# A pooling and attention mixer on 8 cores: far masks queued ahead of the rope products, and the conditioning product on four 32-column quarters of the array

## What is computed

```
shift, scale, gate = split(silu(c) @ w_mod + b_mod)       # w_mod is 1024 x 3072, f32; also for c_ctx
h = rms_norm(x, g_pre) * (1 + scale) + shift               # the same for the context tokens
xa, ga, q, k, v, gb, gm = split(h @ w_in)                  # 1024 x 5632
y_a = pool_mixer(xa) * silu(ga)
y_b = windowed_attention(rope(q), rope(k), v, k_ctx, v_ctx, sink) * silu(gb)
out = (sigmoid(gm_a) * (y_a @ w_a) + sigmoid(gm_b) * (y_b @ w_b)) @ w_out
x_new = x + gate * rms_norm(out, g_post)
```

## Time and profile before

| | us |
|---|---|
| median of 3 runs | 2377.49 (2376.29 to 2379.74) |
| the profiled execution | 2375.37 |
| its span on the slowest core, from the first to the last instruction | 2373.8 |
| spans of all cores | 2366.8 to 2373.8 |
| TensorE busy | 2257.8 |
| VectorE busy | 1595.3 |
| ScalarE busy | 1150.0 |
| GpSimd (POOL) busy | 773.6 |

### The profile page before, as it was taken

How to read it: one execution, slowest core, us unless ns; L and a number is a source line. 1 busy time by engine, 2 the same in 40 slices (tenths; PEclk the granted TensorE clock), 3 DMA queues, 4 the chain that set the end, 5 groups by cost and what they waited for, 6 DMA issues and landing times.

```text
span 2373.8 us, 67010 instructions; the slowest of 8 cores (2366.8 to 2373.8 us)
## 1 busy us (share of the span) xinstructions
PE 2257.8 (95%) x23952; PEld 1336.5 (56%) x23952; DVE 1595.3 (67%) x4226; ACT 1150.0 (48%) x2341; POOL 773.6 (33%) x982
## 2 busy tenths in 40 slices
PE   6789999999999999999999999999999999999998
PEld 1466555555555556556556555555555655655554
DVE  0466776676676676676677667677667667766765
ACT  1255445545545544544544544544554454454453
POOL 0233333233233233233233333333323333333332
PEclk9899999999999999999999999999999999999999
DMA  9981332233232233232234233224223223322212
GB/s 245 222 158 52 69 86 68 68 79 68 70 77 68 70 77 68 70 77 68 70 77 81 69 74 81 70 65 86 68 71 77 68 70 77 73 69 74 72 49 63
DMA packets 234314, 193.77 MB, mean 82 GB/s; under 512 B 197492, under 2 KB 205812, under 8 KB 231432
## 3 DMA queue, kind: packets, MB, share of 16 engines
q1 hardware_dynamic: 231544, 168.45, 29.3%
q0 software_dynamic: 2448, 21.04, 4.8%
HBM read 125.02 MB, written 33.56 MB: 67 GB/s over the span
## 4 chain that ended last, share of the span: by engine, by line
PE 83%; DVE 9%; issue 3%; ACT 2%; DMA 2%; POOL 1%; DVEq 0%; another core or an unknown queue 0%; SPq 0%; ACTq 0%; POOLq 0%
PE pb L581 27%; PE pb L588 22%; PE pb L934 9%; PE pb L876 8%; PE pb L830 5%; PE pb L773 5%; PE pb L868 5%; DMA s_PT<-x 2%; DVE s_hT L540 2%; DVE s_Gb L712 2%; DVE s_yb L839 2%; ACT s_ttmp L711 2%; DVE s_PT L812 1%; PE pb L359 1%; POOL s_mg L880 1%
## 5 line engine op out<-in xcount | busy, mean ns | idle before, releaser
L581 PE MATMUL pb<-s_W,s_hT 128*128 128x512 bf16 (+1 forms) x3584 | 776.4, 366 | 0.0
L588 PE MATMUL pb<-s_hT,s_W 128*128 128x128 bf16 x9216 | 600.3, 220 | 64.0 <-DVE s_hT L540 62.4
L588 PEld LDWEIGHTS pb<-s_hT,s_W 128*128 128x128 bf16 x9216 | 531.3, 98 | 175.7 <-issue 137.9
L802 ACT ACTIVATE s_PT<-pb 128x512 bf16<-128x512 f32 x1024 | 529.0, 608 | 117.5 <-PE pb L773 116.9
L581 PEld LDWEIGHTS pb<-s_W,s_hT 128*128 128x128 bf16 x3584 | 340.0, 98 | 312.6 <-issue 5.3
L857 ACT ACTIVATE s_Tm<-pb 128x512 bf16<-128x512 f32 x256 | 153.2, 599 | 389.3 <-PE pb L581 195.0
L812 DVE TENSOR_TENSOR s_PT<-s_PT,s_maskb 128x512 bf16<-128x512 bf16 (+1 forms) x384 | 296.7, 786 | 45.2 <-ACT s_PT L802 22.8
L880 POOL TENSOR_TENSOR s_mg<-s_ub,s_scr 128x512 bf16<-128x512 f32 x128 | 162.1, 1266 | 341.0 <-DVE s_scr L861 337.4
L690 DVE TENSOR_TENSOR s_scr<-pb,s_ropet 128x512 f32<-128x512 f32 x256 | 165.0, 686 | 133.6 <-PE pb L588 133.6
L876 PE MATMUL pb<-s_wmf,s_ybT 128*128 128x512 bf16 x1024 | 242.6, 380 | 0.0
L839 DVE SCALAR_TENSOR_TENSOR s_yb<-pb,s_small,s_Gb 128x64 bf16<-128x64 f32 x1024 | 220.3, 277 | 29.2 <-DVE s_small L836 2.2
(11 more groups left out here) (125 smaller groups left out, 2461.9 us busy)
## 6 DMA issues: line engine op xcount, KB each, us to landing
s_xr<-x SPq DMA_DIRECT2D x63, 512.0 KB, 4.1
y<-s_xr SPq DMA_DIRECT2D x63, 512.0 KB, 2.8
s_xt<-x SPq DMA_DIRECT2D x62, 512.0 KB, 4.1
s_W<-w_in POOLq DMA_DIRECT2D x10, 1024.0 KB, 31.6
s_ropet<-rope SPq DMA_DIRECT2D x64, 128.0 KB, 2.5
s_wmf<-w_mod SPq DMA_DIRECT2D x2, 2048.0 KB, 13.2
s_W<-w_mod SPq DMA_DIRECT2D x2, 2048.0 KB, 28.1
s_wmf<-w_mod POOLq DMA_DIRECT2D x2, 2048.0 KB, 18.4
```

The costliest lines, as they stand in the source:

```text
L581: E("pe", lambda e, k=k: e.matmul(out=pb[:, c0:c0 + n], lhsT=h[:, k, :], rhs=W[:, wblk, k, c0:c0 + n], start=(k == 0), stop=(k == 7)), rea ...
L588: E("pe", lambda e, c=c, k=k: e.matmul(out=pb[:, c * 128:(c + 1) * 128], lhsT=W[:, wblk, k, c * 128:(c + 1) * 128], rhs=h[:, k, :], start= ...
L802: E("act", lambda e, g=g: e.activation(out=PT[:, jb, g, :], in_=banks[g][0][:, :], func=AF.Exp, scale=0.125), reads=[banks[g][1]], writes= ...
```

## The change

*Masks.* `vis()` is cut in two: `masks()` emits the pending masks, and is now also called between `out_evac` and `norm_sq`. The far masks thus stand on VectorE's list ahead of the rope products of `P_q`; the fifth `vis()` finds none pending. In the periods nothing else moves.

*Conditioning.* `sc` becomes eight groups of 32 columns, of which 4 hold the conditions and the rest zeros from a memset. `mod_mm` makes four products for each k, each with 32 stationary and 128 moving columns, into rows 32j to 32j + 31 of the bank. `mod_row` copies 128 rows of 128 elements, and `mod_fin` has one product with a selection matrix `sel` (built on POOL, in place of `ident4`) instead of four. `gate_block` works on 128 x 128 with biases and weights from a table of 128 x 512 in `ub`, one load of 256 KB instead of four of 8 KB, and makes four stores per block instead of one.

```diff
-        ident4 = sb("ident4", [4, 4], F32)
+        sel = sb("sel", [128, 4, 4], F32)
...
-        sinkb, cT, sc, mT, bmodT, gpreT = [early(n) for n in (16, 32, 32, 64, 24, 8)]
-        brow = [ub[0:4, :], pview(sA, 0, 4, 0, [[1, 512]])]
-        q1f = qT[1][0:4].bitcast(F32)
-        grow = [xr[0:4, 512:1024], AP(q1f.tensor, q1f.offset, [list(q1f.ap[0]), [1, 512]])]
...
+        sinkb, cT, sc, mT, bmodT, gpreT = [early(n) for n in (16, 32, 256, 64, 24, 8)]
+        scv = view(xr, 48, [[32, 8], [1, 4]])
...
-        make_ident(ident4, 4, "ident4")
+        E("pool", lambda e: e.memset(sc, 0.0), writes=[bf("sc")])
+        E("pool", lambda e: e.memset(sel[:], 0.0), writes=[bf("sel")])
+        E("pool", lambda e: e.affine_select(out=sel[:], in_=sel[:], pattern=[[-32, 4], [-1, 4]], compare_op=ALU.not_equal,
+                                            fill=1.0, base=0, channel_multiplier=1),
+          reads=[bf("sel")], writes=[bf("sel")])
...
         def mod_mm(blk):
             pg, pgb = next_bank()
             for k in range(8):
-                E("pe", lambda e, k=k: e.matmul(out=pg[0:4, :], lhsT=sc[:, k * 4:(k + 1) * 4], rhs=wm_rhs(blk, k),
-                                                start=(k == 0), stop=(k == 7)),
-                  reads=wm_bufs(blk) + [bf("sc")], writes=[pgb], inc=(k == 7))
+                for j in range(4):
+                    E("pe", lambda e, k=k, j=j: e.matmul(out=pg[32 * j:32 * j + 32, 0:128], lhsT=sc[:, k * 32:(k + 1) * 32], rhs=wm_rhs(blk, k, j),
+                                                         start=(k == 0), stop=(k == 7)),
+                      reads=wm_bufs(blk) + [bf("sc")], writes=[pgb], inc=(k == 7))
             return pg, pgb
...
         def mod_fin(blk):
...
-            for cc in range(4):
-                ch = blk * 4 + cc
-                E("pe", lambda e, cc=cc, ch=ch: e.matmul(out=psA[:, ch * 4:(ch + 1) * 4], lhsT=mr[:, cc * 128:(cc + 1) * 128],
-                                                         rhs=ident4[:], start=True, stop=True),
-                  reads=[mrb, bf("ident4")], writes=[psAb], inc=(cc == 3))
+            E("pe", lambda e: e.matmul(out=psA[:, blk * 16:(blk + 1) * 16], lhsT=mr, rhs=view(sel, 0, [[1, 16]]), start=True, stop=True),
+              reads=[mrb, bf("sel")], writes=[psAb])
...
         def gate_block(h):
...
-            E("sp", lambda e: e.dma_start(out=ggs_d[:, h * 512:(h + 1) * 512], in_=s[0:BPC, :]), reads=[sb_], writes=[bf(f"ggs{h}")],
-              dma_sem=dsem(f"d_ggs{h}"))
+            for j in range(4):
+                E("sp", lambda e, j=j: e.dma_start(out=ggs_d[:, h * 512 + j * 128:h * 512 + (j + 1) * 128], in_=s[32 * j:32 * j + BPC, 0:128]),
+                  reads=[sb_], writes=[bf(f"ggs{h}{j}")], dma_sem=dsem(f"d_ggs{h}{j}"))
...
-            def vis():
+            def masks():
                 for m in pend:
                     mask(p, m)
                 pend.clear()
+
+            def vis():
+                masks()
                 jb = next(visits, None)
...
             if hasO:
                 out_evac(p - 2, so)
+            masks()
             if nxt:
                 norm_sq()
             q = P_q(p + 1) if hasP else iter(())
...
-        for h in range(2):
-            for dst, b_, src, nm in ((brow[h], [browb[h]], bgate_d, "br"), (grow[h], growb[h], gpost_d, "gr")):
-                E("sp", lambda e, dst=dst, src=src, h=h: e.dma_start(out=dst, in_=src[:, h * 512:(h + 1) * 512].partition_broadcast(4)),
-                  writes=b_, dma_sem=dsem(f"d_{nm}{h}"))
+        ld(ub[:], grow_d, "ub")
```

More of the change, by code:

```diff
@@ L182, in build_program @@
     gpreT_d = din("g_preT", [128, 8])
-    gpost_d = din("g_post", [1, D])
-    bgate_d = din("b_gate", [1, D])
+    grow_d = din("gate_rows", [128, 512])
     pscale_d = din("pool_scale", [1, 512])
@@ L305, in early @@
             return xr[:, a:a + n]
-        sinkb, cT, sc, mT, bmodT, gpreT = [early(n) for n in (16, 32, 32, 64, 24, 8)]
-        brow = [ub[0:4, :], pview(sA, 0, 4, 0, [[1, 512]])]
-        q1f = qT[1][0:4].bitcast(F32)
-        grow = [xr[0:4, 512:1024], AP(q1f.tensor, q1f.offset, [list(q1f.ap[0]), [1, 512]])]
-        browb = [bf("ub"), bf("sA")]
-        growb = [[bf("grow0")], [bf("qT1_0"), bf("qT1_1")]]
-        EARLY = [bf(n) for n in ("sinkb", "cT", "sc", "mT", "bmodT", "gpreT", "grow0")]
+        sinkb, cT, sc, mT, bmodT, gpreT = [early(n) for n in (16, 32, 256, 64, 24, 8)]
+        scv = view(xr, 48, [[32, 8], [1, 4]])
+        EARLY = [bf(n) for n in ("sinkb", "cT", "sc", "mT", "bmodT", "gpreT")]
         def make_ident(t, n, nm):
@@ L335, in wm_bufs, with wm_rhs @@
             return [bf(f"wmf{blk % 2}")] if wm_home[blk][1] is None else [bf(f"W{wm_home[blk][1] + i}") for i in range(2)]
-        def wm_rhs(blk, k):
+        def wm_rhs(blk, k, j):
             t, b0 = wm_home[blk]
-            return t[:, k, :] if b0 is None else f32_at(t, b0 * 2048, k, 512)
+            return t[:, k, j * 128:(j + 1) * 128] if b0 is None else f32_at(t, b0 * 2048 + j * 128, k, 128)
         def load_wmod(blk, q):
@@ L393, in build_program @@
         load_wmod(2, "sp")
-        E("act", lambda e: e.activation(out=sc, in_=cT, func=AF.Tanh, scale=0.5), reads=[bf("cT")], writes=[bf("sc")])
-        E("dve", lambda e: e.scalar_tensor_tensor(out=sc, in0=sc, scalar=1.0, in1=cT, op0=ALU.add, op1=ALU.mult),
+        E("act", lambda e: e.activation(out=scv, in_=view(xr, 16, [[4, 8], [1, 4]]), func=AF.Tanh, scale=0.5), reads=[bf("cT"), bf("sc")], writes=[bf("sc")])
+        E("dve", lambda e: e.scalar_tensor_tensor(out=scv, in0=scv, scalar=1.0, in1=view(xr, 16, [[4, 8], [1, 4]]), op0=ALU.add, op1=ALU.mult),
           reads=[bf("sc"), bf("cT")], writes=[bf("sc")])
-        E("dve", lambda e: e.tensor_scalar_mul(out=sc, in0=sc, scalar1=0.5), reads=[bf("sc")], writes=[bf("sc")])
+        E("dve", lambda e: e.tensor_scalar_mul(out=scv, in0=scv, scalar1=0.5), reads=[bf("sc")], writes=[bf("sc")])
         def mod_end():
@@ L432, in load_gg @@
             E("sp", lambda e: e.dma_start(out=gg[:], in_=ggs_d[b:b + 1, :].partition_broadcast(128)),
-              reads=[bf("ggs0"), bf("ggs1")], writes=[bf("gg")], dma_sem=dsem("d_gg"))
+              reads=[bf(f"ggs{h}{j}") for h in range(2) for j in range(4)], writes=[bf("gg")], dma_sem=dsem("d_gg"))
         TT = BPC * NT
@@ L1187, in rows, with gate_rows @@
         return f(a.reshape(-1, 128, a.shape[1]).transpose(1, 0, 2).reshape(128, -1))
+    def gate_rows(b, g):
+        return f(np.concatenate([np.repeat(v.reshape(2, 4, 1, 128)[h], 32, axis=1).reshape(128, 128) for v in (b, g) for h in range(2)], axis=1))
     b_mod = f(b_mod)[0]
```

16 lines of the change are left out of this document (8 added, 8 removed).

## The result

The changed kernel takes 2269.59 us in the median (2268.75 to 2271.13, 5 runs), the kernel before 2378.26 beside it: a ratio of 0.9547 [0.9533, 0.9561]. That is 108.7 us off, where 74.5 were forecast. The range, 2292 to 2324, does not hold it, although the sign was right. In some runs one die has a lower granted clock, down to 0.81, and takes longer; all ratios, and the times of the experiments, leave those runs out.

A forecast was written before the change was run, and what follows sets the result against it. TensorE, busy 2257.8 of 2373.8 us, was taken as the bound. Loop wait 58.4, clock 4.8, gate blocks 9.1 and period 0 3.6 sum to 75.9 us off; with adjustments for run median and sequence ends, 2303 us, range 2292 to 2324.

The forecast's parts named there:

- the price of the loop's wait: Main loop: TensorE's 62.4 us of waits for VectorE's modulation (L540) shrink to 4 us, 58.4 us off; bounds 31 and 62.4.
- (a): Loop: half the wait stays, as gb product, tanh, L712 and modulations may bind; 2330 to 2335 us, chance 0.13.
- (c): Loop: moving the masks brings nothing; 2365 us with the start's gains alone, 2377 without these; chance 0.03.
- The clock, 4.8 us: Loop: three stretches at the lower granted clock after waits, 1.7 us each, go with the waits; bounds 0 and 5.
- Rival (d): Loop: TensorE, never idle, is granted the lower clock more often; 2407 us with one stretch in each period; chance 0.03.
- The masks' new place: VectorE's gap before the rope products: four far masks at 409 ns each fit there, ending at 1007.5.
- My cover for the delay of the rope products: Loop: rope products start 0.45 us later, but the next `qT` has 12 us of cover, so costed at nothing.
- Late next: Loop: TensorE's own gb product becomes the next late item, with up to 0.1 us of wait left a period.
- The gate blocks, 14.15 to 5.0 us: Start: conditioning blocks 4 and 5 on the chain of waits, quarters side by side, 9.1 us off.
- Rival (b): Start: the gate quarters run serially, 13.7 to 27 us in place of 5.0; 2312 to 2325 us, chance 0.14.
- The rest of the start is worth nothing: Start: faster blocks 0 to 3 and one mod_fin product gain nothing, since the staged x load is the chain there.
- period 0: First period: pv no longer waits for the masks and VectorE's evacuations come earlier, 3.6 us off; bounds 2.0 and 5.5.

The follow-up runs named there:

- the run with eight modulations ahead: Changed kernel with all eight modulations of the next tile emitted ahead of the ga product on VectorE, instead of four ahead and four behind: 2262.35 us, ratio 0.9514.
- the run with the known delay: Changed kernel with two VectorE maxima, results unused, ahead of the last four modulations of a period: 2355.7 us in the median, ratio 0.9908.
- the run with POOL kept busy: Changed kernel with two POOL additions of 512 elements, results unused, put beside the early masks: 2287.64 us in the median, ratio 0.9642.

## Why the prediction was right or wrong

**The failed step is the price of the loop's wait, "58.4 us off" of "62.4".** The mechanism of the loop was right, and the wait went whole; rivals (a) and (c) fell with it. But 62.4 us was never its cost. The idle time of a row counts from the modelled end of the products before it to the first product that follows. It leaves out two things. Sixteen undisturbed products take 0.90 us from start to start (the run with eight modulations ahead), 56 ns each. So TensorE could have issued the fifth 0.23 us after the first, but the row of the first four ends after 0.40 us, and only there the idle time begins: 0.17 us. And the first products behind the wait come at the pace at which VectorE delivers chunks. The trace has four starts at 1026.83, 1027.05, 1027.28 and 1027.50, as far apart as those of the four L540, at 1026.38, 1026.60, 1026.82 and 1027.04; only the other eight are 55 ns apart. That makes 1.17 us from 1026.83 to 1028.00, where twelve at 56 ns take 0.67: 0.50 us. With the idle 1.17 it is 0.17 + 1.17 + 0.50 = 1.84 us. The changed kernel still has 0.12 of such a stall, so the difference of the two stretches is 1.72. My bound of 62.4 at the upper end was therefore no bound, and that put the range wrong. The rows that I had shown give the right number: 1028.00 - 1025.26 = 2.74 us, against 16 products at what an undisturbed row gives. Median against median the segment gave 1.54 us a period, 95.5 us; the run with the known delay shows nearly the same ratio of price to listed wait, 86.8 to 54.8, as the change, 95.5 to 62.4.

**The clock, 4.8 us.** Right, if small (three stretches at 1.7 us are 5.0, a slip of mine). The windows that had 0.96 have 1.00:

```profile
980.00:1020.00 40.00, 40.00 (x428) 23.48 (x421) 25.71 (x71) 22.37 (x48) 13.46 (x19) 1.00 0.27 64
```

Before, three segments of the loop took 7.7 to 7.8 us, 1.9 to 2.0 over the median and not 1.7; after, the longest is 4.62 us. The run with the conditioning alone has four of 7.8 to 7.9, so they go with the waits. Rival (d), the lower clock in every period, found no support: TensorE is at 97% and all eight cores have a granted clock of 0.984 to 0.989. The Trainium skill (TensorE: Matmul & The Clock Gate, "Seeing it yourself") expects 13/16 there; the profiled executions disagree again.

**The masks' new place.** Right: they are in the gap before the rope products, and end 1.49 us behind the far exponentials (1025.65, against 1022.95 + 1.21 = 1024.16), where I had 1.0. I took 409 ns for each from the earlier trace rows, and line 811 has a median of 426; in the row of four it is 485 each. The second L860 starts 7.4 us behind the exponentials, as forecast (1013.9 - 1006.48), and waits for POOL's sum, as forecast. The first waits for POOL's q combination (0.93 us), where I had only its own product. My cover for the delay of the rope products counted `qT` alone; through POOL's list the delay also reaches the second L860, as the run with POOL kept busy shows (masks 0.67 us longer, second L860 0.61 later). It cost little because the masks were short. The Trainium skill (GPSIMD Engine Reference, "1. Specifications") says that GpSimd's SBUF interfaces contend with VectorE instructions that have two SBUF inputs; the masks are such, and 0.48 us alone against 1.3 beside L694 agrees.

**Late next.** I named TensorE's own gb product and left 0.1 us a period for it. That was of the right size, but it does not appear as a wait: it is the 0.12 us that the run with eight modulations ahead took off.

**The gate blocks, 14.15 to 5.0 us.** Measured 4.11, so 10.0 us off in place of 9.1. Rival (b), serial quarters, fell for the kernel's order, and the run that orders them so shows 11.75, below the 13.7 of my serial end (a quarter of 442 ns is 110 and not 107, which makes that end 14.1). The estimate that mattered was the far-score row as the nearest. The Trainium skill (TensorE: Matmul & The Clock Gate, "The mechanism") would have weight loads overlap only where the row group differs. Here all four quarters have the same rows, and the traces disagree: loads and products of different column quarters overlap, and the order of the loop alone makes 2.9 times.

**"The rest of the start is worth nothing", and period 0.** The sum of both was roughly right and the ledger not. Period 1 came 13.6 us earlier (145.3 to 131.7 in the medians of the cores; forecast 9.1 + 3.6 = 12.7), but period 2 only 7.3 (177.1 to 169.8): 6.3 us were given back. The step that failed is that the rope table's load has ample slack. The slack was VectorE's lateness, and the change took that away while the load could not be faster; a wait of 4.1 us and a stretch at the lower clock behind it came in its place. With the conditioning alone, a small store of the gate was on the chain as well: it took 14.51 us, and VectorE was idle for the last 0.45 of them. I had priced the stores at 2 us on SP's queue and not at the buffer that they hold. The cover of w_o held.

So the terms, forecast and measured: loop wait and clock 63.2 and 98; start 12.7 and 7 to 8; together 75.9 and 106 in the profiled executions.

## What to carry to other kernels

Price a recurring wait of a pipelined engine from start to start over the whole stretch around it, against the same stretch undisturbed, and not by the idle time ahead of one row: the part before the wait ends sooner than modelled, and the part behind it runs at its supplier's pace. A stall can be there with no idle row at all, so a stretch that takes more than its count times the pace of the engine is worth an edit, as the last 7 us here. And where a phase is bound by full DMA engines, ask of each load whose slack is another engine's lateness what it will do once that engine is on time. Price the wait with what follows it: 4.1 us of idle TensorE cost 7.0 here, with the lower clock behind it.

## What the runs showed of the hardware that was not expected

Four f32 products of 32 stationary and 128 moving columns, on the four column quarters of the array with the same 128 rows, took 32 ns per pass in alternation and 92 ns when each quarter got its eight products, sixteen passes, in a row. A store of 1 KB took 14.5 to 15.5 us to release its buffer while the DMA engines were full, about as long as a load of 128 KB (17.0 us). A VectorE minimum of 128 x 512 bf16 took 0.48 us with POOL idle and 1.3 us beside a POOL instruction on f32. After a single wait of 4.13 us TensorE's granted clock was 0.56 for the next 7 us.
